# A two-block model: the delta net's chain starts 35 phases behind the forget gate's, and ScalarE copies four kinds of tiles out of PSUM

## The chip, the cores and the metric

The kernel runs on one NeuronCore of one Trainium2 chip. The metric is the device time of one launch in microseconds (us), here the median of three runs. A profiled execution gives one more time, with the span of the core and the start and duration of every instruction.

## What is computed

The reference runs two transformer blocks over 256 tokens of width 2048 in fp32. The first block is attention beside a diagonal state space model and a feed-forward net. The second block mixes three branches: a long convolution, a gated linear recurrence ("hgrn2", here the **forget gate**) and a **gated delta net**. Both recurrences have 8 heads of 128 by 128 and run in two directions, over 256 tokens of context and 256 tokens of the grid:

```python
lf_f, k_f = forget(f_f, lb_f)            # log decay and key of the forget gate
o_f, s_f = _gla_scan(qh, k_f, ih, lf_f, states[0])
o_b, s_b = _gla_scan(_flip(qh), _flip(k_b), _flip(ih), _flip(lf_b), states[1])
o = _rmsnorm_2(o_f + _flip(o_b), norm_w) * jax.nn.sigmoid(heads(g))
...
o_f, s_f = _delta_scan(q, k, v, g_f, jax.nn.sigmoid(b_f), states[0])
o_b, s_b = _delta_scan(_flip(q), _flip(k), _flip(v), _flip(g_b), _flip(jax.nn.sigmoid(b_b)), states[1])
o = _rmsnorm_2(o_f + _flip(o_b), norm_w) * jax.nn.silu(zh)
```

Both scans are done by blocks of 128 tokens: products inside a block are joined over levels of halves (64, 32, ... 1 tokens), then a state goes from block to block.

## The kernel before, in words

The program writes each engine's instruction list by hand. SyncE loads weights in tiles of 256 KB into a ring of 8 slots. Most of the time goes to projections; the change touches one stage, `heads2`, from 2533 to 3502 us of the span.

In `heads2` two chains run side by side, `forget_*` (functions for TensorE, VectorE and ScalarE) and `delta_*`. A chain is a Python generator per engine, and every `yield` ends a **phase**. `lockstep` takes one phase of each generator in turn, so it fixes the order in which every engine gets the pieces of the two chains; within a phase the forget gate's piece stands first, the end of the head before ahead of it, and both directions (r = 0, 1) follow one another. Each engine executes its list strictly in that order and waits on semaphores for the others. Nothing waits for a phase as such.

- One head of the forget gate takes 52 phases. I number them p0 to p51. Phases p0 to p10 are the **start**: bounds, the decay's reciprocals (all of p2), scans (p4), keys, their transpose and the diagonal product (p9, p10). Then 7 levels of 5 phases, then the state's steps from p46.
- One head of the delta net takes 49 phases, q0 to q48. q0 to q8 are its **opening** (products and masks); q8 to q32 are 6 **levels** of 4 phases. In a level TensorE makes `left` (8 fp32 products 128x128, 16 instructions in the trace), ScalarE keeps it in `y`, TensorE makes `both` (16 products 128x64, 32 instructions), VectorE subtracts (L1747, L1749) and masks (L1739) for the next level. q32 to q48 are the **tail**: the sides, `wide` and its negation, and four times `solved`, new values `vn`, state.
- At a head's end `end_*` normalizes its output; it runs in the first three phases of the next head.
- `beside` puts pieces of ordinary projections between the phases, the **background**: 8 groups of 36 pieces (32 of them are two products `L589`, 4 are for ScalarE's stores), spread over 414 phases.

`chain` runs the 8 heads one after the other. The delta net's chain is 18 phases late at head 0. As its head is 3 phases shorter, it is 15 late at head 1 and 3 early at head 7.

Of the kernel before, what the change touches and what calls it, by code (L numbers as in the profile page):

```python
# [10 lines left out]
ACT = mybir.ActivationFunctionType  # L11
AX = mybir.AxisListType

P = 128
# [191 lines left out]
def lockstep(strands):  # L206
    strands = list(strands)
    while strands:
        for s in list(strands):
            try:  # L210
                next(s)
            except StopIteration:
                strands.remove(s)
        yield

def beside(strand, pieces, background):
    total = sum(n for _, n in background)
    gens = [g for g, _ in background]
    done = given = 0
    for _ in strand:  # L220
        done += 1
        while gens and given < total * done / pieces:
            try:
                next(gens[0])
                given += 1
            except StopIteration:
                gens.pop(0)
    for g in gens:
        for _ in g:
            pass  # L230
# [1188 lines left out]
def tiles(b, n=NT):  # L1419
    return b[:, 0:n * P].rearrange("p (j t) -> p j t", j=n)  # L1420

def flat(t):
    return t.rearrange("p j t -> p (j t)")
# [54 lines left out]
def forget_vector(k, r, head):  # L1478
    v, s, po = k.nc.vector, k.s, k.acc[2 + r]
    h, after, before, end = hg_views(k, r)  # L1480
    fwd = r == 0
    ev = lambda name, *x: ("hg_" + name, r, head, *x)
    f, kk, e1, ks, cm, qe, att, m, st = (h[n] for n in ("f", "k", "e1", "ks", "cum", "qe", "att", "lev", "st"))
    lbc, lb1c = k.lb[:, r, head:head + 1], k.lb1_[:, r, head:head + 1]
    own = Own(k)
# [36 lines left out]
    own(v.tensor_tensor(ks, ks, kk, ALU.mult), *ev("keys"))  # L1522
    yield
    yield
    v.wait_ge(*s.at(*ev("keys_t")))
    own(v.tensor_copy(e1, tiles(po)), *ev("kst"))
    if not fwd:
        own(v.tensor_tensor(qe, end[:, 0:2, :].broadcast_to((P, 2, P)), before[:, 0:2, :], ALU.subtract), *ev("query_sums"))
    yield
# [38 lines left out]
def forget_scalar(k, r, head):  # L1568
    a, s = k.nc.scalar, k.s
    h, after, before, end = hg_views(k, r)  # L1570
    fwd = r == 0
    ev = lambda name, *x: ("hg_" + name, r, head, *x)
    yield
    a.wait_ge(*s.at(*ev("bounded")))
    a.activation(h["e1"], h["e1"], ACT.Exp).then_inc(*s.made("scalar_done", *ev("exped")))
    yield
    yield
    a.wait_ge(*s.at(*ev("scaled")))
    a.activation(h["f"], h["f"], ACT.Ln).then_inc(*s.made("scalar_done", *ev("logs")))
    yield  # L1580
    yield
    a.wait_ge(*s.at(*ev("sums")))
    a.activation(h["ks"], h["ks"], ACT.Exp).then_inc(*s.made("scalar_done"))
    a.activation(h["eend"], h["cum"][:, :, P], ACT.Exp).then_inc(*s.made("scalar_done", *ev("decays")))
    yield
    yield
    yield
    if fwd:
        a.activation(h["qe"], after[:, 0:2, :], ACT.Exp).then_inc(*s.made("scalar_done", *ev("query_decays")))
    else:  # L1590
        a.wait_ge(*s.at(*ev("query_sums")))
        a.activation(h["qe"], h["qe"], ACT.Exp).then_inc(*s.made("scalar_done", *ev("query_decays")))
    yield
    yield
    for level in range(7):
        yield
        a.wait_ge(*s.at(*ev("spans", level)))
        a.activation(h["lev"], h["lev"], ACT.Exp).then_inc(*s.made("scalar_done", *ev("span_decays", level)))
        yield
        yield  # L1600
        yield
        yield
    for _ in range(6):
        yield
# [85 lines left out]
def delta_vector(k, r, head):  # L1690
    v, s = k.nc.vector, k.s
# [4 lines left out]
    own = Own(k)  # L1696
# [57 lines left out]
    own(v.tensor_tensor(x, k.kt_h, col(ek), ALU.mult), *ev("sides"))  # L1754
    yield
    yield
    v.wait_ge(*s.at(*ev("wide")))
    own(v.tensor_scalar(y, tiles(b0), -1.0, None, ALU.mult, ALU.bypass), *ev("negated"))
    for n, j in enumerate(order_of(r)):
        yield  # L1760
        v.wait_ge(*s.at(*ev("solved", n)))
        own(v.tensor_copy(vn, b1[:, 0:P]), *ev("new", n))
        yield
        if n < 3:
            yield
            v.wait_ge(*s.at(*ev("added", n)))
            if n == 0:
                own(v.tensor_copy(st, b1[:, P:2 * P]), *ev("state", n))
            else:
                own(v.scalar_tensor_tensor(st, st, el[:, j:j + 1], b1[:, P:2 * P], ALU.mult, ALU.add), *ev("state", n))  # L1770
            yield

def delta_scalar(k, r, head):
    a, s = k.nc.scalar, k.s
    d, (g_, gc_, be, eg, el, ek), b0, b1 = dn_views(k, r)
    ev = lambda name, *x: ("dn_" + name, r, head, *x)
    yield
    yield
    yield
    yield  # L1780
    a.wait_ge(*s.at(*ev("logs")))
    a.activation(d["dec"], d["dec"], ACT.Exp).then_inc(*s.made("scalar_done"))
    a.activation(d["qe"], tiles(b0, 2), ACT.Exp).then_inc(*s.made("scalar_done"))
    a.activation(eg, gc_, ACT.Exp).then_inc(*s.made("scalar_done"))
    a.activation(el, el, ACT.Exp).then_inc(*s.made("scalar_done"))
    a.activation(ek, ek, ACT.Exp).then_inc(*s.made("scalar_done", *ev("decays")))
    yield
    yield
    yield
    yield  # L1790
    for level in range(5, -1, -1):
        yield
        yield
        a.wait_ge(*s.at(*ev("left", level)))
        a.activation(d["y"], tiles(b0), ACT.Copy).then_inc(*s.made("scalar_done", *ev("kept", level)))  # L1795
        yield
        yield
    yield
    yield
    for n in range(4):  # L1800
        yield
        yield
        if n < 3:
            yield
            yield
# [32 lines left out]
def hg_start_scalar(k, head):  # L1838
    a, s, b = k.nc.scalar, k.s, head % 2
    a.wait_ge(*s.at("hg_loaded", head))  # L1840
    if head:
        a.wait_ge(*s.at("hg_q", head - 1))
    a.activation(k.hsg, flat(k.hq[b]), ACT.Sigmoid).then_inc(*s.made("scalar_done"))
    a.activation(k.hgt[b], k.hgt[b], ACT.Sigmoid).then_inc(*s.made("scalar_done", "hg_sig", head))
    for _ in range(8):
        yield
    if head < 7:
        hg_load(k, head + 1)
# [11 lines left out]
def hg_start_vector(k, head):  # L1860
    v, s, q = k.nc.vector, k.s, flat(k.hq[head % 2])
    yield
    v.wait_ge(*s.at("hg_sig", head))
    v.tensor_tensor(q, q, k.hsg, ALU.mult).then_inc(*s.made("vector_done", "hg_q", head))
    yield
    v.wait_ge(*s.at("hg_v_t", head))
    v.tensor_copy(flat(k.hvt), k.acc[2][:, :]).then_inc(*s.made("vector_done", "hg_vt", head))
    yield

def dn_start_scalar(k, head):  # L1870
# [60 lines left out]
def chain(k, name, start, strand, end, delay=0):  # L1931

    for _ in range(delay):
        yield
    for head in range(8):
        before = [end(k, name, head - 1)] if head else []
        yield from lockstep(before + [strand(k, r, head) for r in range(2)] + [start(k, head)])
    yield from end(k, name, 7)

def heads2(k, hg_start, forget, dn_start, delta, end, whole):  # L1940
    chains = [chain(k, "hg", hg_start, forget, end), chain(k, "dn", dn_start, delta, end, 18)]
    beside(lockstep(chains), 414, [(whole(k, g), 36) for g in k.some("read", 11, 12) + k.some("gates", *range(6))])

def heads2_tensor(k):
    heads2(k, hg_start_tensor, forget_tensor, dn_start_tensor, delta_tensor, end_tensor, whole_tensor)
# [475 lines left out]
```

## Time and profile before

| | |
|---|---|
| median of 3 runs | 4931.92 us (4926.59 to 4939.75) |
| the profiled execution | 4934.87 us, its span 4933.4 us |
| TensorE matmuls busy | 4316.6 us, 87% |
| VectorE busy | 2810.2 us, 57% |
| ScalarE busy | 1548.4 us, 31% |
| `heads2` | 2533 to 3502 us |
| SyncE's weights | 597 MB in the launch, 34 MB of them in `heads2` |

Busy time is the sum of an engine's instructions. It is a mean over stages with different limits, so what matters here is read inside `heads2`. Matmuls overlap with the next one, so that a group of n is shorter than n single ones.

### The profile page before, as it was taken

Reading aid. Unit: us, or ns where it says so; the run is one execution under the profiler, and the core shown is the slowest. Engines: PE = TensorE matmul, PEld = TensorE weight load, DVE = VectorE, ACT = ScalarE, POOL = GpSimd, SP = SyncE. Lnnn points to the kernel's source line nnn. Section 1 sums busy time; section 2 is a strip of 40 time slices with the busy share of each in tenths; the row PEclk is TensorE's granted clock in tenths of the full one; section 3 lists DMA queues with packets and bytes.
Section 4 is the critical chain, followed back from the end, with each engine's and each line's share of the span. In section 5 each row is a group of like instructions: output and inputs, shape, how many; then the busy total and the mean of one; then the engine's idle time right before and its main releaser. Section 6 shows DMA issues by size and latency. Waiting matters only on the chain.

```text
span 4933.4 us, 69710 instructions
## 1 busy us (share of the span) xinstructions
PE 4316.6 (87%) x28096; PEld 3667.4 (74%) x28096; DVE 2810.2 (57%) x5619; ACT 1548.4 (31%) x2683; POOL 0.2 (0%) x4
## 2 busy tenths in 40 slices
PE   7598899699999989999877778777778897999997
PEld 7333223689999978889767777777645797999997
DVE  4756444566556542234557777777632476655654
ACT  3211111444444432234122222222100243444442
POOL 0000000000000000000000000000000000000000
PEclk9799999899999999999789899998989999999999
DMA  5344555346565654457451112121422463655653
GB/s 174 96 147 147 169 163 155 121 153 190 187 187 180 192 149 120 115 147 208 120 150 51 55 52 58 50 58 40 127 70 75 156 200 116 192 187 185 186 188 112
DMA packets 383056, 669.52 MB, mean 136 GB/s; under 512 B 43897, under 2 KB 77402, under 8 KB 382220
## 3 DMA queue, kind: packets, MB, share of 16 engines
q1 hardware_dynamic: 327168, 595.74, 40.2%
q10 hardware_dynamic: 55564, 69.31, 4.3%
q8 instruction: 221, 3.62, 0.3%
q14 instruction: 103, 0.84, 0.1%
HBM read 634.87 MB, written 29.46 MB: 135 GB/s over the span
## 4 chain that ended last, share of the span: by engine, by line
PE 63%; DVE 13%; issue 2%; ACT 2%; DMA 1%; ACTq 0%; DVEq 0%
PE acc L547 13%; PE acc L549 12%; PE acc L548 12%; PE acc L589 8%; PE bank L548 2%; PE bank L547 2%; PE bank L549 2%; PE bank L1654 2%; PE bank L1663 2%; PE bank L1661 1%; ACT weights_hi L511 1%; PE bank L2130 1%; DVE arena L1493 1%; PE acc L1462 1%; PE bank L734 1%
## 5 line engine op out<-in xcount | busy, mean ns | idle before, releaser
L526 DVE TENSOR_TENSOR weights_lo<-weights_ring,weights_hi 128x512 fp32r<-128x512 f32 x1600 | 1094.1, 691 | 1022.5 <-ACT weights_hi L511 1020.9
L511 ACT ACTIVATE weights_hi<-weights_ring 128x512 fp32r<-128x512 f32 x1600 | 994.3, 630 | 1078.8 <-PE acc L549 882.3
L548 PE MATMUL acc<-arena_halves,weights_hi 128*128 128x256 f32 (+2 forms) x3136 | 916.3, 292 | 0.0
L547 PE MATMUL acc<-arena_halves,weights_lo 128*128 128x256 f32 (+1 forms) x2944 | 860.4, 292 | 21.7 <-DVE weights_lo L526 12.2
L549 PE MATMUL acc<-arena_halves,weights_hi 128*128 128x256 f32 (+1 forms) x2944 | 858.8, 292 | 0.0
L547 PE MATMUL acc<-moving_halves,weights_lo 128*128 128x256 f32 (+1 forms) x2816 | 792.1, 281 | 73.0 <-DVE weights_lo L526 72.3
L549 PE MATMUL acc<-moving_halves,weights_hi 128*128 128x256 f32 (+1 forms) x2816 | 786.6, 279 | 0.0
L548 PE MATMUL acc<-moving_halves,weights_hi 128*128 128x256 f32 x2624 | 731.4, 279 | 0.0
L548 PEld LDWEIGHTS acc<-arena_halves,weights_hi 128*128 128x128 f32 x3136 | 590.5, 188 | 12.1
L547 PEld LDWEIGHTS acc<-moving_halves,weights_lo 128*128 128x128 f32 x2816 | 535.7, 190 | 81.6 <-DVE weights_lo L526 53.6
L589 PE MATMUL acc<-moving,weights_ring 128*128 128x256 f32 x2304 | 581.2, 398 | 10.4 <-ACT arena L692 9.3
L547 PEld LDWEIGHTS acc<-arena_halves,weights_lo 128*128 128x128 f32 x2944 | 553.3, 188 | 36.9 <-DVE weights_lo L526 13.0
L549 PEld LDWEIGHTS acc<-arena_halves,weights_hi 128*128 128x128 f32 x2944 | 553.6, 188 | 13.6
L549 PEld LDWEIGHTS acc<-moving_halves,weights_hi 128*128 128x128 f32 x2816 | 535.4, 190 | 0.0
L589 PEld LDWEIGHTS acc<-moving,weights_ring 128*128 128x128 f32 x2304 | 442.1, 201 | 95.7 <-issue 30.5
L548 PEld LDWEIGHTS acc<-moving_halves,weights_hi 128*128 128x128 f32 x2624 | 497.9, 190 | 0.0
L1088 PE MATMUL acc<-weights_ring,cc 128*2 128x512 f32 x768 | 370.6, 620 | 12.2 <-ACT mods_row L1101 12.1
L1088 PEld LDWEIGHTS acc<-weights_ring,cc 128*2 128x2 f32 x768 | 55.5, 85 | 247.6 <-issue 221.9
L548 PE MATMUL bank<-arena_halves,weights_hi 128*128 128x256 f32 (+2 forms) x640 | 209.3, 327 | 0.0
L547 PE MATMUL bank<-arena_halves,weights_lo 128*128 128x512 f32 (+1 forms) x512 | 171.8, 336 | 0.0
L549 PE MATMUL bank<-arena_halves,weights_hi 128*128 128x512 f32 (+1 forms) x512 | 171.0, 334 | 0.0
L1795 ACT ACTIVATE arena<-bank 128x512 f32<-128x512 f32 x96 | 56.6, 596 | 236.7 <-PE bank L1654 236.7
(422 smaller groups left out, 4830.9 us busy)
## 6 DMA issues: line engine op xcount, KB each, us to landing
weights_ring<-in_w_in SPq DMA_DIRECT2D x624, 256.0 KB, 2.7
weights_ring<-in_w_ff SPq DMA_DIRECT2D x512, 256.0 KB, 3.0
weights_ring<-in_w_ada SPq DMA_DIRECT2D x384, 256.0 KB, 2.9
weights_ring<-in_w_up SPq DMA_DIRECT2D x256, 256.0 KB, 2.9
weights_ring<-in_w_down SPq DMA_DIRECT2D x256, 256.0 KB, 3.2
weights_ring<-in_w_out SPq DMA_DIRECT2D x128, 256.0 KB, 3.2
weights_ring<-in_w_branch SPq DMA_DIRECT2D x96, 256.0 KB, 3.3
s_state<-arena ACTq DMA_DIRECT2D x36, 256.0 KB, 2.8
```

The source lines that it names most:

```text
L511: a.activation(whi, k.slot(g.ring0 + kc), ACT.Copy).then_inc(*s.made("scalar_done", "high", n))
L526: v.tensor_tensor(wlo, k.slot(g.ring0 + kc), whi.bitcast(F32), ALU.subtract).then_inc(*s.made("vector_done", "low", n))
L547: pe.matmul(g.out[m], wlo[:, cols], xhi, start=first, stop=False, skip_group_check=g.shared)
L548: pe.matmul(g.out[m], whi[:, cols], xlo, start=False, stop=False, skip_group_check=g.shared)
L549: mm = pe.matmul(g.out[m], whi[:, cols], xhi, start=False, stop=last, skip_group_check=g.shared)
L589: mm = pe.matmul(g.out[m], k.slot(g.ring0 + kc)[:, m * P:(m + 1) * P], g.x(kc), start=kc == 0 and m % 2 == 0, stop=last, skip_group_check= ...
L734: mm = pe.matmul(k.bank[0][:, 0:n], k.c("ones"), squares[:, c, :], start=c == 0, stop=c == chunks - 1)
L1088: mm = pe.matmul(g.out[0], ccv[:, kc, :], k.slot(g.ring0 + kc), start=kc == 0, stop=kc == g.kchunks - 1)
L1462: mm = pe.matmul(po[:, P * j:P * j + P], h["lev"][:, j, :], h["lev"][:, j, :], start=True, stop=True)
L1654: mm = pe.matmul(b0[:, P * j:P * j + P], mt[:, j, :], x[:, j, :], start=True, stop=True)
L1663: mm = pe.matmul(b1[:, 64 * j:64 * j + 64], y[:, j, :], level_columns(xt[:, j, :], level, 1 - r), start=True, stop=True)
L1795: a.activation(d["y"], tiles(b0), ACT.Copy).then_inc(*s.made("scalar_done", *ev("kept", level)))
```

## The change

Two things change, both in `heads2`.

The chains: the delta net's starts 35 phases late rather than 18, and `chain` fills each head up to 51 phases. The forget gate's heads have 52 and aren't filled. So the delta net is 35 - h phases late at head h, 28 at the last. The last phase of the stage is number 446 rather than 419, and the background is spread over 444.

The copies: the transposed keys (`kst`, 16 times 128x512), the transposed values (`hg_vt`, 8 times 128x512), the negated product (`negated`, 16 times 128x512) and the new values (`new`, 64 times 128x128) are taken out of PSUM by ScalarE's `Copy` and no longer by VectorE.

```diff
@@ forget_vector
     yield
-    v.wait_ge(*s.at(*ev("keys_t")))
-    own(v.tensor_copy(e1, tiles(po)), *ev("kst"))
     if not fwd:
@@ forget_scalar
+    a.wait_ge(*s.at(*ev("keys_t")))
+    a.activation(h["e1"], tiles(k.acc[2 + r]), ACT.Copy).then_inc(*s.made("scalar_done", *ev("kst")))
     if fwd:
@@ delta_vector
-    v.wait_ge(*s.at(*ev("wide")))
-    own(v.tensor_scalar(y, tiles(b0), -1.0, None, ALU.mult, ALU.bypass), *ev("negated"))
     for n, j in enumerate(order_of(r)):
         yield
-        v.wait_ge(*s.at(*ev("solved", n)))
-        own(v.tensor_copy(vn, b1[:, 0:P]), *ev("new", n))
         yield
@@ delta_scalar
+    a.wait_ge(*s.at(*ev("wide")))
+    a.activation(d["y"], tiles(b0), ACT.Copy, scale=-1.0).then_inc(*s.made("scalar_done", *ev("negated")))
     for n in range(4):
         yield
+        a.wait_ge(*s.at(*ev("solved", n)))
+        a.activation(d["vn"], b1[:, 0:P], ACT.Copy).then_inc(*s.made("scalar_done", *ev("new", n)))
@@ hg_start_scalar
-    for _ in range(8):
+    yield
+    yield
+    a.wait_ge(*s.at("hg_v_t", head))
+    a.activation(flat(k.hvt), k.acc[2][:, :], ACT.Copy).then_inc(*s.made("scalar_done", "hg_vt", head))
+    for _ in range(6):
         yield
@@ hg_start_vector
-    v.wait_ge(*s.at("hg_v_t", head))
-    v.tensor_copy(flat(k.hvt), k.acc[2][:, :]).then_inc(*s.made("vector_done", "hg_vt", head))
@@ chain
-        yield from lockstep(before + [strand(k, r, head) for r in range(2)] + [start(k, head)])
+        phases = 0
+        for _ in lockstep(before + [strand(k, r, head) for r in range(2)] + [start(k, head)]):
+            phases += 1
+            yield
+        for _ in range(51 - phases):
+            yield
@@ heads2
-    chains = [chain(k, "hg", hg_start, forget, end), chain(k, "dn", dn_start, delta, end, 18)]
-    beside(lockstep(chains), 414, [(whole(k, g), 36) for g in k.some("read", 11, 12) + k.some("gates", *range(6))])
+    chains = [chain(k, "hg", hg_start, forget, end), chain(k, "dn", dn_start, delta, end, 35)]
+    beside(lockstep(chains), 444, [(whole(k, g), 36) for g in k.some("read", 11, 12) + k.some("gates", *range(6))])
```

VectorE's list around the forget gate's phase p2 of head 1 (L1506 is the end of p2's second direction), of the kernel before:

```order
L1506 TENSOR_TENSOR arena<-arena 128x512
L1867 COPY arena<-acc 128x512
L1762 COPY arena<-bank 128x128 x2
L1510 SCALAR_TENSOR_TENSOR arena<-arena 128x512
L1513 SCALAR_TENSOR_TENSOR arena<-arena 128x128 x4
L1516 TENSOR_TENSOR arena<-arena 128x512
L1510 SCALAR_TENSOR_TENSOR arena<-arena 128x512
L1513 SCALAR_TENSOR_TENSOR arena<-arena 128x128 x4
L1518 COPY arena<-arena 128x512
L1770 SCALAR_TENSOR_TENSOR arena<-arena,bank 128x128 x2
```

and of the change:

```order
L1506 TENSOR_TENSOR arena<-arena 128x512
L1747 TENSOR_TENSOR arena<-arena,bank 128x32x8
L1749 TENSOR_TENSOR arena<-arena,bank 128x32x8
L1739 TENSOR_TENSOR arena<-arena,consts_sb 128x512
L1747 TENSOR_TENSOR arena<-arena,bank 128x32x8
L1749 TENSOR_TENSOR arena<-arena,bank 128x32x8
L1739 TENSOR_TENSOR arena<-arena,consts_sb 128x512
L1510 SCALAR_TENSOR_TENSOR arena<-arena 128x512
L1513 SCALAR_TENSOR_TENSOR arena<-arena 128x128 x4
L1516 TENSOR_TENSOR arena<-arena 128x512
```

Before, the delta net's tail stood beside the start (new values L1762, state L1770); now a step of its levels does.

TensorE's list at the same head, from the transpose of the values (phase p0) on. Before:

```order
L1856 MATMUL acc<-consts_sb,arena 128x128 x4
L589 MATMUL acc<-moving,weights_ring 128x256 x2
L1674 MATMUL bank<-arena 128x128
L1676 MATMUL bank<-arena 128x128
L1674 MATMUL bank<-arena 128x128
L1676 MATMUL bank<-arena 128x128
L589 MATMUL acc<-moving,weights_ring 128x256 x2
L1686 MATMUL bank<-arena 128x128 x2
```

and now:

```order
L1860 MATMUL acc<-consts_sb,arena 128x128 x4
L1654 MATMUL bank<-arena 128x128 x8
L1661 MATMUL bank<-arena 128x64 x4
L1663 MATMUL bank<-arena 128x64 x4
L1661 MATMUL bank<-arena 128x64 x4
L1663 MATMUL bank<-arena 128x64 x4
L589 MATMUL acc<-moving,weights_ring 128x256 x2
L1654 MATMUL bank<-arena 128x128 x8
L589 MATMUL acc<-moving,weights_ring 128x256 x2
L1661 MATMUL bank<-arena 128x64 x4
```

Short products of the tail's solving stood behind the transpose; now it is the delta net's `left` (L1654) and `both` (L1661, L1663).

ScalarE's list in the delta net's tail of head 0, of the change (L1598 is the exponential of the forget gate's levels, L1801 the copy of new values, L1834 to L1836 the loads of the next head):

```order
L1797 ACTIVATE arena<-bank 128x512 x2
L1801 ACTIVATE arena<-bank 128x128 x2
L1834 DMA arena<-s_kf 128x512
L1834 DMA arena<-s_qf 128x256
L1834 DMA arena<-s_kt 128x512
L1835 DMA arena<-s_vt 128x512
L1836 DMA mixed<-s_read 128x256
L1598 ACTIVATE arena<-arena 128x256 x2
L1801 ACTIVATE arena<-bank 128x128 x4
L1598 ACTIVATE arena<-arena 128x256 x2
```

Before, L1797 and L1801 weren't in it. ScalarE's list as a whole now has 124 table loads (`ACT_TABLE_LOAD`) where it had 100, since the two chains' different functions alternate more often.

## Rows read from the trace of the kernel before

**Rows 1.** Windows: the stage; busy us of each engine, clock, DMA share, GB/s
```profile
2533.00:3502.00 969.00, 745.09 (x5216) 692.65 (x5216) 733.49 (x1848) 263.50 (x505) 0.00 (x0) 0.90 0.19 55
```
**Rows 2.** Timeline, VectorE: first instruction (L1487) and p10 (L1535) of forget-gate heads 0, 1, 7
```profile
2541.27 0.76 DVE L1487 TENSOR_SCALAR arena<-arena 128x512 f32<-128x512 f32 x2
2570.52 0.42 DVE L1535 TENSOR_TENSOR arena<-acc,consts_sb 128x256 f32<-128x256 f32 x1 [0.99 <-PE acc L1453]
...
2648.55 0.75 DVE L1487 TENSOR_SCALAR arena<-arena 128x512 f32<-128x512 f32 x2
2681.82 0.41 DVE L1535 TENSOR_TENSOR arena<-acc,consts_sb 128x256 f32<-128x256 f32 x1
...
3374.78 0.75 DVE L1487 TENSOR_SCALAR arena<-arena 128x512 f32<-128x512 f32 x2
3424.74 0.42 DVE L1535 TENSOR_TENSOR arena<-acc,consts_sb 128x256 f32<-128x256 f32 x1
```
**Rows 3.** Timeline, VectorE: delta net's q0, q8, q32 (head 1), q32, q0 (heads 6, 7), stage's end
```profile
2690.18 2.12 DVE L625 TENSOR_SCALAR arena<-arena 128x4 f32<-128x4 f32 x10
...
2710.58 0.68 DVE L1736 TENSOR_TENSOR arena<-consts_sb,bank 128x512 f32<-128x512 f32 x1
...
2760.35 0.69 DVE L1753 TENSOR_TENSOR arena<-arena 128x512 f32<-128x512 f32 x1
...
3345.04 0.69 DVE L1753 TENSOR_TENSOR arena<-arena 128x512 f32<-128x512 f32 x1
...
3367.09 2.12 DVE L625 TENSOR_SCALAR arena<-arena 128x4 f32<-128x4 f32 x10
...
3495.51 0.42 DVE L1912 COPY arena<-acc 128x256 f32<-128x256 f32 x1 [1.06 <-PE acc L1470]
...
3500.95 0.42 DVE L1922 TENSOR_TENSOR moving<-arena 128x256 f32<-128x256 f32 x1
```
**Rows 4.** Timeline: phase p2 of head 2 on VectorE, and TensorE's first row behind it
```profile
2775.22 0.42 DVE L1491 TENSOR_SCALAR arena<-arena 128x512 f32<-128x512 f32 x1
...
2790.30 0.68 DVE L1867 COPY arena<-acc 128x512 f32<-128x512 f32 x1
...
2791.24 1.22 PE L1686 MATMUL bank<-arena 128*128 128x128 f32 x4 [16.74 <-DVE arena L1762]
```
**Rows 5.** Windows: a stretch in head 7's start, and one in its levels
```profile
3382.00:3390.00 8.00, 0.00 (x0) 0.00 (x0) 7.72 (x11) 3.44 (x11) 0.00 (x0) 0.50 0.00 0
...
3436.00:3448.00 12.00, 12.00 (x93) 11.52 (x91) 5.35 (x16) 2.79 (x7) 0.00 (x0) 1.00 0.21 55
```
**Rows 6.** Timeline, TensorE: `left` of both directions twice, and a quarter of `both`
```profile
2604.35 1.98 PE L1654 MATMUL bank<-arena 128*128 128x128 f32 x16
...
3413.34 3.78 PE L1654 MATMUL bank<-arena 128*128 128x128 f32 x16 [4.36 <-DVE arena L1739]
...
3455.89 1.06 PE L1661 MATMUL bank<-arena 128*128 128x64 f32 x8
```
**Rows 7.** Single lines: copies out of PSUM on VectorE and ScalarE (ns min/median/max)
```profile
L1526 DVE COPY arena<-acc x16: 681/682/692, 2566.7 to 3420.0; 128x512 f32<-128x512 f32 x16
L1762 DVE COPY arena<-bank x64: 281/291/293, 2652.3 to 3486.7; 128x128 f32<-128x128 f32 x64
L1783 ACT ACTIVATE arena<-bank x16: 363/367/367, 2582.5 to 3382.9; 128x256 f32<-128x256 f32 x16
L1795 ACT ACTIVATE arena<-bank x96: 578/597/601, 2596.2 to 3461.4; 128x512 f32<-128x512 f32 x96
```
**Rows 8.** Timeline, ScalarE: a table load and the instruction behind it
```profile
2541.97 1.28 ACT L1575 ACT_TABLE_LOAD   x1
...
2543.26 1.15 ACT L1575 ACTIVATE arena<-arena 128x512 f32<-128x512 f32 x2
```
**Rows 9.** Timeline, TensorE: the forget gate's first two level products, alone in the stage
```profile
2573.36 1.05 PE L1462 MATMUL acc<-arena 128*128 128x128 f32 x8
...
2576.84 1.05 PE L1462 MATMUL acc<-arena 128*128 128x128 f32 x8
```

## The prediction

> **What bounds the kernel now.** I read the page first, then only the stage that is touched. The stage takes 969 us, a fifth of the launch; TensorE is busy for 745 us of it, VectorE for 733 and ScalarE for 264 [rows 1]. So neither of the two busy engines is full: they take turns. The windows show how. In the forget gate's start VectorE is full and TensorE stands still; in the levels TensorE is full and VectorE is half idle [rows 5]. The cause is phase p2: one block of 15.1 us on VectorE (2790.30 less 2775.22), and as both chains share its in-order list, the delta net's small step behind it arrives late and TensorE sits idle for 16.7 us [rows 4]. To the stage it thus matters what the other chain has to do while VectorE is in the start, and whether TensorE is given work that needs no VectorE.
>
> The timeline gives the price of each piece by what lay beside it:
> - start, p0 to p10: 29.3 us alone (head 0), 33.3 over the delta net's tail (head 1), 50.0 over its opening (head 7) [rows 2]. The last heads are dear because both VectorE-heavy parts meet there.
> - opening, q0 to q8, over levels: 20.4 us, with the end of the head before. Levels, q8 to q32, over levels: 49.8 us, 2.07 a phase, with TensorE full [rows 3, 5]. Tail, q32 to the next q0, over levels: 22.1 us for 17 phases [rows 3].
>
> **The change part by part.** The chains first, as they carry the sum. With a delay of 35 - h the forget gate's p0 stands at the delta net's q17 + h. So now its start lies over *levels* of the delta net at every head, the opening lies over the forget gate's levels, and so does the tail. TensorE-heavy and VectorE-heavy parts are paired, and openings no longer meet starts.
>
> *One period of the delta net*, 51 phases, put together from these pieces:
> 1. opening over levels: 20.4 us, unchanged.
> 2. 24 phases of levels, 10 of them under the forget gate's start, so 14 at 2.07: 29.0.
> 3. tail with the two phases of filling, 19 phases at 22.1/17: 24.6.
> 4. the start over ten phases of levels, which no row shows. Bound below: VectorE's work alone. From head 1's 33.3 us I take off 1.8 for the copies that leave (two of keys and one of values, 0.68 long and about 0.6 from start to start [rows 7]) and 3.5 for the tail's own steps, and add 2.5 level steps at 2.9 (six instructions of the sizes 128x256 and 128x512), so 35.2. Bound above: 48, a little under head 7's 50.0. My value: 6 for p0 and p1 with the end, 15.1 for p2, and then TensorE. The order listing shows that it can issue `left` and `both` ahead of the block's end, but a second `left` and `both`, a third `left`, the keys' transpose, the diagonal and three background pieces stand behind it. Eight instructions take 1.06 us, 0.9 where the next ones follow [rows 6], so these are 1.8, 3.5, 1.8, 0.9, 0.9 and 2.7: 11.6 us. It comes back at half clock: while it stood idle the granted clock was 0.50, the lower level of 1.2 GHz [rows 5], and `left` took 3.78 us then against 1.98 at the full clock [rows 6]; that adds about 3. With hand-overs between three engines some 19. Sum: 40. I take 40, nearer to the lower end, since that end is worked out from a row of the same start, while the upper comes from an opening that isn't there any more.
> 5. The background is thinner, 288/444 of a piece a phase for 288/414: 0.04 us a phase where TensorE is full, so -1.0.
>
> That is 113.0. *The copies*: 16 x 0.68 for keys, 8 x 0.68 for values, 16 x 0.68 for the negation and 64 x 0.29 for new values leave VectorE, 46 us by durations [rows 7]. Those in the start are counted above. The others lie in the tail over levels, which TensorE's list fills, so VectorE's relief is worth nothing there. ScalarE gains about as much: 0.60 for 128x512, and for 128x128 between 0.19 and the 0.37 of 128x256 [rows 7], I take 0.25, so 40 us more on 264 of 969. As a link of the chain that is the same as before within 0.1 us. What is new is the queue: new values now wait behind the forget gate's exponentials, five load issues at q36 and any table load. 24 more of these at 1.28 us are 31 us of ScalarE. Eleven stand at the levels' exponential, where the delta net's opening meets levels, which VectorE bounds, and the consumer is two phases (over 4 us) later, so I charge only 1.0 us a period. Sum: **114.0 us a period**. Before it was 112.8 (676.9 us from head 1's q0 to head 7's [rows 3]), but for 49 phases rather than 51.
>
> The table loads are also where a rule speaks against this. The row shows the next activation 1.29 us after the load began, so nothing lies behind the load itself [rows 8]. The Trainium skill, "ScalarE: Activation LUTs", section "What ACT_TABLE_LOAD costs", gives 1.28 us plus a drain of 1.38, 2.66 us for a switch of sets; by an estimate from that page the 24 more would be 64 us of ScalarE rather than 31. The trace agrees on the load and shows no drain behind it.
>
> *The edges*, where extra phases cost. The forget gate now runs alone for 35 phases: the start 29.3 - 0.6, then five levels at 3.7 (its products are 3.5 us apart when alone [rows 9], with thin cover), 18.5: **47.1 us** before the delta net begins. The last head has opening 20.4, levels 49 (a quarter of them alone, so slightly under 49.8), tail alone 18.5 (22.1 less four level products of the forget gate) and the last normalization 6 (3495.5 to 3501.4 [rows 3]): **94 us**. Head 0's opening has no end beside it: -3.8.
>
> *Sum*: 47.1 + 7 x 114.0 + 94 - 3.8 = 935.3 us from the first L1487. Before it was 3501.4 - 2541.3 = 960.1 [rows 2, 3]. The difference is -24.8 us, against the profiled execution's 4934.9: **4910 us**. The median of the three runs is 3 us lower than the profiled execution, so it would be 4907; I stay with the sum's own base.
>
> The fixed loads ahead of the next head (q36 and p8) have over 15 us to land; if they were late, VectorE would wait at L1487 or at `scaled`. I see no case for it, as DMA is busy for a fifth of the stage [rows 1].
>
> **The rivals.** The total is 137.3 + 7 x period, and each us on the start is 7 us on the kernel.
>
> *A. The start over levels is VectorE's work and nothing else*, 35.2 us: TensorE hides wholly in it. For it: VectorE is 97% busy in the start [rows 5]. Against: a level goes through VectorE twice in these phases, and the half clock. -25 - 34 = -59 us: 4876.
>
> *B. The block stops the levels (the other side: slower).* In the start both chains step through VectorE's list. If each level step waits for the block and for the scans of p4 as well, so that `left` and `both` are hardly issued under p2, TensorE has 16.9 us to do behind the block at a partly halved clock, and the start is 48 us, as dear as over an opening. +56 - 25 = +31: 4966. It decides from a start of 45.7 us on, where the kernel is slower by 0.3%. For it: 16.7 us of idle TensorE at a similar place [rows 4]. Against: the order listing, with 5.3 us of products ahead of the block's end.
>
> *C. ScalarE's queue.* If all 24 table loads lie on the chain, 31 us come on top less the 7 that I charge: nearly 4934, no change. For it: new values and exponentials alternate on one in-order list in the tail. Against: ScalarE is idle for 73% of the stage [rows 1]. By the page's 2.66 us instead it would be 64 - 7 - 25 = +32 us, which the row on the load speaks against.
>
> *D. The change does not do what it says*: overlapped phases stay as long as they are. From head 1's start to head 7's there were 312 phases in 726 us, 2.33 each [rows 2]; 383 of these, 47 ahead and 36 behind give 975, +15 us: 4950. That is B in a milder form (a start near 46) and shares its chance.
>
> **How the numbers follow.** A measurement of this kernel can tell about 0.3% from no change, 15 us. My forecast (a start of 38 to 43 us, so 4896 to 4931) has 0.50; A 0.17; C 0.12; B with D 0.21. Within the forecast's band about 7 parts in 10 are faster by over 15 us (0.36), the rest the same. Faster: 0.36 + 0.17 + 0.02 of C = 0.55. Same: 0.14 + 0.10 of C = 0.24. Slower: 0.21. The range goes from 4873, just under A, to 4958, which holds D and leaves out the upper half of B.
>
> **What would show it.** The profile after should have: L1487 to L1533 (p10) near 40 us at heads 1 to 7, all alike, where it was 33 to 50; the delta net's period near 114; its first opening about 47 us after the first L1487; TensorE's idle behind p2 down from 16.7 to about 10 us. VectorE's busy time in the stage falls by about 46 us and ScalarE's rises by about 70. I am wrong if the starts take over 46 us (B), if the tail over levels takes over 28 us with TensorE waiting for ScalarE's L1801 (C), or if the opening or the plain levels change their price at all, as I carried those over from other pairings.

## The result, and the profile after

The change makes the kernel **0.24% slower**: 4949.01 us, median of 8 runs (4945.34 to 4955.16), against 4936.9 us of the kernel before on the same chip. The ratio is 1.0024, 95% interval 1.0012 to 1.0035. The profiled execution has a span of 4944.6 us, 11.2 more than before. I had forecast 25 us less.

Of the span's 11.2 us, 10.7 lie in the stage. Windows of the kernel after, the stage (columns as in [rows 1]):

```profile
2533.00:3511.00 978.00, 769.17 (x5216) 711.81 (x5216) 693.14 (x1742) 330.28 (x635) 0.00 (x0) 0.89 0.19 55
```

From the first L1487 to the end of the last normalization it took 960.1 us before and takes 970.8 now (2542.39 to 3513.16), +10.7. The copies moved as announced: VectorE's busy time fell by 40 us and ScalarE's rose by 67 [rows 1]. TensorE has the same 5216 instructions, and its busy time is 24 us more; its mean granted clock is 0.89 where it was 0.90.

The timeline of VectorE after the change shows where the phases went (L1533 is p10, L625 q0, L1736 q8, L1753 q32, as in [rows 2, 3]):

```profile
2542.39 0.76 DVE L1487 TENSOR_SCALAR arena<-arena 128x512 f32<-128x512 f32 x2
...
2590.27 2.12 DVE L625 TENSOR_SCALAR arena<-arena 128x4 f32<-128x4 f32 x10
...
2628.01 0.76 DVE L1487 TENSOR_SCALAR arena<-arena 128x512 f32<-128x512 f32 x2
...
2821.45 2.12 DVE L625 TENSOR_SCALAR arena<-arena 128x4 f32<-128x4 f32 x10
2840.70 0.69 DVE L1736 TENSOR_TENSOR arena<-consts_sb,bank 128x512 f32<-128x512 f32 x1
...
2865.95 0.76 DVE L1487 TENSOR_SCALAR arena<-arena 128x512 f32<-128x512 f32 x2
...
2909.13 0.42 DVE L1533 TENSOR_TENSOR arena<-acc,consts_sb 128x256 f32<-128x256 f32 x1
...
2913.95 0.69 DVE L1753 TENSOR_TENSOR arena<-arena 128x512 f32<-128x512 f32 x1
...
2938.74 2.12 DVE L625 TENSOR_SCALAR arena<-arena 128x4 f32<-128x4 f32 x10
...
3353.69 0.76 DVE L1487 TENSOR_SCALAR arena<-arena 128x512 f32<-128x512 f32 x2
...
3419.45 2.12 DVE L625 TENSOR_SCALAR arena<-arena 128x4 f32<-128x4 f32 x10
```

Read the same way at all heads, with the forecast beside it (us; means over seven heads):

| | before | forecast | after |
|---|---|---|---|
| forget gate alone, first L1487 to first q0 | 35.3 | 47.1 | 47.9 |
| start, p0 to p10, heads 1 to 7 | 41.0 | 40 | 40.8 |
| opening, q0 to q8 (with head 0's shorter one) | 24.2 | 19.9 | 19.6 |
| levels, q8 to q32, the start in them | 50.0 | 68.0 | **72.5** |
| tail, q32 to the next q0 | 38.7 | 24.6 + 1.0 | **26.4** |
| period of the delta net | 112.9 | 113.5 | **118.45** |
| last head, its q0 to the end | 134.3 | 94 | 93.7 |

(Before, the start lay over other parts, so that only the sums of its rows compare with the new ones. The forecast's 114.0 was to be shortened by 3.8 us once, for head 0's opening, which is 113.5 as a mean.) The edges and the mean start came out within 1 us. But the starts are not all alike, as I had forecast: they take 36.9 to 44.8 us, where it was 33.3 to 50.0. The period is 5 us over, and seven of these are the 35 us by which the sum failed.

The waits of TensorE in the stage (engine, tile, line, for whom: us in total, times, longest), first before:

```profile
PE bank L1639 <- DVE arena L1722: 61.5, 8, 25.0
PE bank L1897 <- DVE mixed L1914: 23.5, 8, 17.3
PE bank L1674 <- DVE arena L1770: 20.6, 3, 16.3
...
PE bank L1686 <- DVE arena L1762: 17.8, 2, 16.7
PE bank L1674 <- DVE arena L1768: 16.7, 1, 16.7
PE bank L1682 <- DVE arena L1762: 15.7, 2, 15.5
```

and after:

```profile
PE bank L1654 <- DVE arena L1739: 74.9, 18, 17.0
PE bank L1661 <- ACT arena L1791: 42.0, 7, 16.8
PE bank L1639 <- DVE arena L1722: 18.1, 8, 3.4
```

The openings' wait fell from 61.5 to 18.1 us, as meant. The longest idle time of TensorE around p2 has mostly changed its name: it was 15.5 to 17.3 us at heads 1 to 5, mostly in front of the tail's steps, and 25.0 and 22.0 at heads 6 and 7, in front of openings. Now it is 11.6, 17.0, 16.8, 15.4, 10.7, 14.6 and 16.8 us at heads 1 to 7, in front of `left` (L1654) or `both` (L1661): 14.7 as a mean. I had forecast 10. The block of head 3 and what follows, kernel after, timeline:

```profile
2874.82 0.42 DVE L1491 TENSOR_SCALAR arena<-arena 128x512 f32<-128x512 f32 x1
...
2889.90 0.69 DVE L1510 SCALAR_TENSOR_TENSOR arena<-arena 128x512 f32<-128x512 f32 x1
2890.01 0.63 ACT L1577 ACTIVATE arena<-arena 128x512 f32<-128x512 f32 x1 [6.91 <-DVE arena L1506]
2890.55 1.07 ACT L1791 ACTIVATE arena<-bank 128x512 f32<-128x512 f32 x2
2891.18 1.97 PE L1661 MATMUL bank<-arena 128*128 128x64 f32 x8 [16.84 <-ACT arena L1791]
```

The block is 15.08 us as before. ScalarE keeps `left` in L1791 only behind the logarithm L1577, which waits for the block's end; so `both`, which I had counted as issued under the block, starts behind it. It is the same at head 7, and at head 2 even `left` stands behind the block. At the other heads the products do run beside it: 36 of TensorE's instructions start in the block at head 1, 40 at heads 4 and 5, 12 at head 6, and TensorE idles behind them. Windows of the block of head 3 and of the 4 us behind it:

```profile
2874.82:2889.90 15.08, 0.00 (x0) 0.00 (x0) 14.60 (x20) 0.63 (x1) 0.00 (x0) 0.58 0.00 0
2891.00:2895.00 4.00, 3.82 (x18) 3.82 (x19) 3.90 (x11) 3.57 (x6) 0.00 (x0) 0.50 0.10 33
```

TensorE does nothing in this block, and behind it runs at the granted clock of 0.50, the lower level of 1.2 GHz.

### The profile page after: what moved, and what is told of

Its sections match the earlier page's. It is cut to its first block and busy times, and to the rows that moved or that the text cites. A ratio compares the mean times of both kernels' runs of the same rounds, so it can differ in the third digit from the quotient of the medians.

```text
span 4944.6 us, 69734 instructions
## 1 busy us (share of the span) xinstructions
PE 4341.5 (88%) x28096; PEld 3690.2 (75%) x28096; DVE 2772.5 (56%) x5515; ACT 1613.8 (33%) x2811; POOL 0.2 (0%) x4
## 5 line engine op out<-in xcount | busy, mean ns | idle before, releaser
L547 PEld LDWEIGHTS acc<-arena_halves,weights_lo 128*128 128x128 f32 x2944 | 552.5, 188 | 37.1 <-DVE weights_lo L526 13.3
L1654 PE MATMUL bank<-arena 128*128 128x128 f32 x768 | 108.9, 299 | 74.9 <-DVE arena L1739 74.9
```

The lines of the kernel that those rows point to most:

```text
L547: pe.matmul(g.out[m], wlo[:, cols], xhi, start=first, stop=False, skip_group_check=g.shared)
L1654: mm = pe.matmul(b0[:, P * j:P * j + P], mt[:, j, :], x[:, j, :], start=True, stop=True)
```

## Experiments

Thirteen kernels ran. "Period" is again the delta net's mean from q0 to q0, in each kernel's own trace.

### Which half of the change costs: e1_chains, e2_copies

e1 has the chains alone, e2 the copies alone.

```diff
e1: chain(..., 18) -> chain(..., 35), fill to 51 phases, background over 444; all copies on VectorE
e2: keys, values, negated product, new values on ScalarE; delay 18, no fill, 414
```

> The chains alone (35 phases behind, heads filled to 51, background over 444); all four copies stay on VectorE. Theory 1 (block and clock: in the start TensorE idles some 15 us behind p2 and comes back at half clock with dense level work; the copies matter little): ratio to before 1.001 to 1.005, delta-net period 117 to 120 us, still a long wait of TensorE behind p2. Theory 2 (ScalarE's queue: the moved copies hold up the tail and the levels): the period falls to 114 or under, ratio 0.993 to 0.998. Both: tail over levels 26.5 us if the chains do it, 24.6 if the copies did.

> The four copies alone, with the old delay of 18, no filling, background over 414. Theory 1: 12 to 15 us of VectorE relief lie in the starts, where VectorE is full, so ratio 0.996 to 0.999. Theory 2: ratio 1.002 to 1.006, with TensorE waiting for ScalarE's new values.

Measured: e1 4944.66 us, ratio 1.0021 (1.0010 to 1.0033), period 119.0. e2 4938.63 us, ratio 1.0001 (0.9992 to 1.0010), period 112.9, as before.

So the chains carry the loss, and no worth of the copies is told from nothing, where theory 1 had 0.996 to 0.999 for them: with e1's chains they take 1.1 us from the levels (73.6 to 72.5) and give 1.0 back in the tail (25.4 to 26.4).

### ScalarE's queue: e3_vn_vector, e4_scalar_order

e3 is the change with the new values taken out by VectorE again. In e4 ScalarE's pieces of a phase come in the other order, the delta net's first:

```diff
-    beside(lockstep(chains), 444, ...)
+    beside(lockstep(chains[::-1] if whole is whole_scalar else chains), 444, ...)
```

> The change, with only the new values (64 copies 128x128) back on VectorE. Theory 1: same time as the change within 0.1% (ratio to before 1.001 to 1.004), as the tail's list is TensorE's. Theory 2: the tail over levels falls from 26.5 to about 24.5 us, 15 us less than the change.

> The change, with ScalarE's list alone taking the delta net's piece of a phase before the forget gate's. At the heads where keeping `left` shares phase p3 with the logarithm, it no longer stands behind it, so TensorE's wait of up to 16.8 us for L1791 shrinks to under 5. Theory 1: those are 2 or 3 of 7 starts, TensorE then gets `both` under the block: 5 to 8 us each, ratio to the change 0.996 to 0.999. If in-phase order on ScalarE matters everywhere (theory 2): more than 25 us less than the change.

Measured: e3 4944.07 us, 1.0016 (1.0006 to 1.0026), period 118.0, tail 25.5. e4 4949.59 us, 1.0025 (1.0015 to 1.0036), period 119.1. The waits of TensorE in e4:

```profile
PE bank L1654 <- DVE arena L1739: 123.0, 18, 19.1
PE bank L1639 <- DVE arena L1722: 22.0, 8, 5.2
```

The wait for L1791 is gone from the list, and the one for VectorE has grown from 74.9 to 123.0 us, against 116.9 for the two together. At heads 3 and 7 `both` is now issued in the block (25 and 29 instructions start there, where none did), and the next `left` waits for the block's end instead; at heads 1 and 5 only 4 do, where it was 36 and 40. The 5 to 8 us a head that I had expected didn't come: the order on ScalarE decides which product waits, and hardly for how long. By e3 the new values on ScalarE (rival C) cost 0.8 us in the tail and 0.4 in the period.

### TensorE's clock: e5_clock_kept, e8_clock_kept_to_end

Products of constants into a free accumulator are put behind p2 on TensorE, to keep its clock up: 22 a head in e5, by head 27 to 40 in e8. The output does not use them.

```diff
@@ hg_start_tensor
+    yield
+    if head:
+        pe.wait_ge(*s.at("hg_o_mean", head - 1))
+    for _ in range((40, 28, 38, 38, 38, 27, 33, 38)[head]):
+        pe.matmul(k.acc[3][:, 0:T], k.ident, k.c("masks")[:, 0:T], start=True, stop=True)
+    yield
```

> The change, plus 22 products 128x256 of constants in TensorE's list at each p2, into a bank that nobody reads before it is overwritten: about 9.7 us of work that needs nothing of VectorE, in a stretch where TensorE otherwise idles 15 us. It does no useful work, it only keeps the clock. Theory 1a (the half clock behind the block is what makes the 24 phases of levels 72 us instead of 68): q8 to q32 with a start falls by 3 to 4 us, the period to about 115, ratio to before 0.996 to 0.999. Theory 1b (the idle is only the hand-over between three engines, the clock is hidden): period stays at 118 or rises, ratio 1.002 to 1.004.

> The change with dummy products behind p2 on TensorE, 27 to 40 of them by head, enough to keep TensorE at work until the block on VectorE ends (in e5_clock_kept they ended some 7 us before it, and the first group of L1661 behind still took 1.97 us and the seam was unchanged, so that run did not test the clock). Theory 'clock' (part of the long seam is the half clock after TensorE's idle): the groups of 16 products at L1654 behind the block take about 2.0 us and not 3.5 to 3.8, q8 to q32 falls from 72.5 to 68 or 69 us, period from 118.5 to 114 or 115, time 0.994 to 0.998 of the kernel before. Theory 'order of work' (VectorE's own instructions and the waits between the two chains set the seam, and the clock is hidden by them): the groups are short again but q8 to q32 stays within 1 us of 72.5 and the time within 0.1% of the change's, 1.002 to 1.003.

e5 took 4947.54 us, 1.0019 (1.0009 to 1.0029), with the change's own period, 118.45. At head 2 its products ended 6 us before the block did, and the clock had fallen again, so e5 tested nothing. The first `left` behind the block of head 2, on TensorE's timeline, in the kernel after:

```profile
2772.79 3.78 PE L1654 MATMUL bank<-arena 128*128 128x128 f32 x16 [17.04 <-DVE arena L1739]
```

The same in e5:

```profile
2766.58 3.78 PE L1654 MATMUL bank<-arena 128*128 128x128 f32 x16 [7.48 <-DVE arena L1739]
```

And in e8, where it comes as one group for each direction:

```profile
2765.90 1.16 PE L1654 MATMUL bank<-arena 128*128 128x128 f32 x8 [0.58 <-DVE arena L1739]
```

In e8 each direction's 8 instructions take 1.16 us, at the full clock. Still: e8 4942.44 us, 1.0016 (1.0007 to 1.0024), period 118.48 against the change's 118.45. But that doesn't show that the clock is hidden, since e8 kept it at some heads only. The next `left` of the same head, in e8:

```profile
2775.36 3.78 PE L1654 MATMUL bank<-arena 128*128 128x128 f32 x16 [0.73 <-DVE arena L1739]
```

It runs at the lower level: behind short waits of TensorE the clock fell 10 us after the block instead of in it. In the kernel after, this `left` took twice 1.16 us. Windows from the block's end to p10, heads 2 and 7, first in the kernel after:

```profile
2771.34:2787.01 15.67, 13.52 (x86) 12.89 (x87) 12.92 (x30) 7.53 (x16) 0.00 (x0) 0.78 0.17 54
3377.72:3398.45 20.73, 18.49 (x104) 17.42 (x104) 14.85 (x34) 7.23 (x14) 0.00 (x0) 0.72 0.10 26
```

and in e8:

```profile
2764.45:2782.54 18.09, 15.20 (x91) 13.38 (x90) 12.87 (x30) 8.00 (x16) 0.00 (x0) 0.81 0.24 74
3373.10:3390.45 17.35, 14.88 (x108) 13.10 (x106) 14.76 (x34) 7.23 (x14) 0.00 (x0) 1.00 0.12 32
```

Where the clock stayed at 1.00 (heads 4, 6, 7), this stretch is 1.2, 0.8 and 3.4 us shorter than in the change, and at head 3 (0.90 for 0.71) 1.5. Where it fell again (heads 1, 2, 5) the stretch is 1.6, 2.4 and 0.4 us longer. Over the seven heads it is 131.2 us in e8 and 133.5 in the change. So e8 shows that this filler buys nothing, and leaves open what a clock kept to the end would be worth.

### Filling the block: e6_background_in_block, e7_before_background_in_block

If TensorE idles for 15 us a head beside a block of VectorE, work that needs no VectorE belongs there. e6 (the change) and e7 (the kernel before) give 16 of a head's 36 background pieces at once at p2, the other 20 spread over 416 phases:

```diff
-def beside(strand, pieces, background):
+def beside(strand, pieces, background, bulk=0):
...
-        while gens and given < total * done / pieces:
+        now = min(bulk * ((done - 3) // 52 + 1), 8 * bulk)
+        while gens and given < now + (total - 8 * bulk) * done / pieces:
```

> The change, with the background laid differently: 16 of the 36 pieces of a head go to the forget gate's p2 (14 us of TensorE work that needs no VectorE), the other 20 are spread over its 52 phases. Theory 1: it keeps the clock as well and takes 0.26 us a phase out of the levels that fill TensorE; the period falls from 118.4 to 108 to 112, ratio 0.987 to 0.993. Theory 1b: only the thinner background counts, 5 to 6 us a period, ratio 0.994 to 0.997. If the weights' ring of 8 slots can't feed it: TensorE waits for weights in p2 and nothing is won.

> The kernel before (delay 18, copies on VectorE), with the same layout of the background. TensorE's idle behind p2 (16.7 us) is filled; the levels lose 0.24 us a phase, 24 phases: 5 to 6 us a period, and 3 us of half clock. Ratio 0.990 to 0.995. If the layout is worth more to the change (whose levels lie beside the start) than to this one, then the chains' shift was right and only the block's idle spoiled it; if it is worth the same, the shift stays a loss of 0.2%.

Measured: **e6 4868.25 us, 0.9854** (0.9839 to 0.9868); e7 4887.05 us, 0.9889 (0.9873 to 0.9904). The period falls from 118.45 to 108.3 and from 112.9 to 106.2. Both gain more than expected (0.987 to 0.993 and 0.990 to 0.995). The change's sign has turned with the layout: with the block filled in both kernels it is 19 us faster (4868.25 against 4887.05), where without that it was 12 slower.

### The rest of that layout: e9_chains_bulk16, e10_bulk20, e11_bulk20_vn_vector

e9 is e1 (copies on VectorE) with 16 pieces at p2; e10 the change with 20; e11 is e3 with 20.

> The chains alone (all copies on VectorE) with 16 of the 36 background products of a head given at p2: tells what the copies are worth once the block is filled. e6_background_in_block, with the copies on ScalarE, gave 4868 us, ratio 0.985. If the copies are worth nothing here too (levels +1.1, tail -1.0 us a period, as without the filled block) it is at 4866 to 4871. If VectorE's instructions bind more once TensorE no longer starves, the copies' 5.7 us of VectorE's work a head show and this run is 10 to 40 us slower than 4868. If the new values on ScalarE cost more than the others bring, it is faster than 4866.

> The change with 20 instead of 16 of the 36 background products of a head given at p2. In the 16 case TensorE was still idle for some us behind them. Theory 'cover': more of the block is filled, each head gains another 1 to 2 us: 4850 to 4862 us, ratio 0.981 to 0.984. Rival 'overrun': the eviction of the 20 products on ScalarE or their columns on TensorE reach past the end of the block and hold the seam back: 4870 to 4885.

> As e10_bulk20, but the new values are taken out of the bank by VectorE (the rest of the copies by ScalarE). The tail was 0.9 us a head shorter so without the filled block (e3_vn_vector), for 0.1% in all. If this holds here, 4 to 8 us faster than e10_bulk20; if VectorE's 24 extra instructions bind, 3 to 8 us slower.

Measured, on one chip (before: 4932.48 us): e9 4869.59 us, 0.9868 (0.9854 to 0.9881), period 109.3; **e10 4857.18 us, 0.9846** (0.9832 to 0.9860), period 108.7; e11 4858.56 us, 0.9851 (0.9831 to 0.9872), period 108.6. The intervals of e9 and e6 overlap, so the 0.14% between them, which would be the copies' worth here, isn't told from nothing. Nor is the place where the new values are taken out (64 instructions, not 24), where 4 to 8 us were expected. e10's 20 pieces are not told apart from e6's 16 by the intervals; its starts are 1.8 us shorter (37.9 against 39.7), its tails 1.2 longer, and its stage is as long (887.0 against 886.8 us). Windows of the block of the same head as above, in e10:

```profile
2845.19:2860.27 15.08, 15.08 (x71) 13.29 (x70) 14.60 (x20) 0.63 (x1) 0.00 (x0) 1.00 0.58 148
```

The block takes 15.08 us beside a full TensorE too, and the granted clock stays at 1.00.

### Is it the background or the phases: e12_no_background, e13_before_no_background

Both kernels with all 288 pieces behind the stage, so that only the two chains are in it.

```diff
-    beside(lockstep(chains), 444, ...)
+    beside(lockstep(chains), 444000, ...)
```

> The change with the 288 projection pieces of the stage all behind it rather than beside it. Only the two chains remain in the stage; the time as a whole must be longer, since the projections are no longer hidden. Read is the period of the delta net, against the same edit of the kernel before (e13). Theory 'background' (the two chains alone pair as well as forecast; what was missed is that projection pieces stand in TensorE's way in more phases than before): the period here is at most 2 us longer than e13's, for 51 phases against 49, e.g. 100 against 98. Rival 'phases' (the overlapped start is dear in itself, for instance because the levels go through VectorE behind the block): the period stays 4 to 6 us longer than e13's, as it is with the background (118.45 against 112.93).

> The kernel before with the 288 projection pieces behind the stage. Gives the delta net's period without background, 49 phases: with 36 pieces a head it is 112.93 us, with 16 of them in the block 106.2. Both theories expect 95 to 102 us here; the difference to e12_no_background decides between them (up to 2 us, or 4 to 6). Time as a whole longer than before: 288 pieces at about 0.97 us are 280 us, less what the stage gets shorter (8 times 11 to 15 us).

The delta net's first and last q0 in e12, from VectorE's timeline:

```profile
2580.61 2.12 DVE L625 TENSOR_SCALAR arena<-arena 128x4 f32<-128x4 f32 x10
...
3339.28 2.12 DVE L625 TENSOR_SCALAR arena<-arena 128x4 f32<-128x4 f32 x10
```

The same two in e13:

```profile
2574.59 2.12 DVE L625 TENSOR_SCALAR arena<-arena 128x4 f32<-128x4 f32 x10
...
3297.81 2.11 DVE L625 TENSOR_SCALAR arena<-arena 128x4 f32<-128x4 f32 x10
```

A seventh of each difference is the period: 108.4 us for 51 phases in e12, 103.3 for 49 in e13. The difference is 5.1 us, almost the 5.5 with the background. So the theory "background" falls and "phases" holds: the two chains alone cost 5 us more a period, two phases longer, when paired so, where 1.2 was forecast (114.0 against 112.8). The clock is not the same in the two: the mean granted clock from the first L1487 to the end of the last normalization is 0.80 in e12 and 0.83 in e13, so that a part of the 5 us may be the clock's. (As a whole: e12 5110.96 us, 1.0336, 1.0321 to 1.0352; e13 5097.27, 1.0325, 1.0304 to 1.0346.) The stage without background is 10.1 us longer than e13's, against the 10.7 with it.

These two runs also say what the background costs. Spread over the phases its 36 pieces take 10.1 us of a period of the change (118.45 less 108.4) and 9.6 of the kernel before. In e6 the period is as long with all of its background as without any: 108.3, and the stage is 886.8 us against 891.2. In e7 2.9 us a period remain. By the stage, the change was 10.7 us longer than the kernel before and is now 22.3 shorter (886.8 against 909.1). Of these 33 us, 24 are the period's and 8 the last head's, which fell from 93.7 to 83.5 us in the change and from 134.3 to 131.8 in the kernel before.

Two things beside the filled block are in that comparison. The granted clock is higher with the background: its mean over the stage is 0.94 in e6 against 0.80 in e12, so "as long as without" is a net result. And the layout takes table loads away: ScalarE's list has 124 in the change and 102 in e6, but 100 in both the kernel before and e7. The 22 loads are 28 us of ScalarE at 1.28 each, 3.5 us a head, as much as e6's period gained beyond e7's (10.1 less 6.7). So no run shows whether the filled block alone turns the sign. e10, with 114 loads and 4 more pieces in the block, has the same stage as e6.

## Why the prediction was wrong

**What held.** The lead of 47.1 us (47.9), the opening over levels (20.4, with head 0's 19.9; 19.6), the last head (94; 93.7), the start (40; 40.8), and that nothing outside the stage moves. A part of the mechanism was right as well: openings no longer meet starts, and the last head is 40 us shorter. That all starts would be alike was not: they spread over 8 us, half as far as before.

**What failed is the sum for one period**, by 5 us, in two of its steps:

1. *"24 phases of levels, 10 of them under the forget gate's start, so 14 at 2.07: 29.0"*, with the 1.0 of step 5 off: 28.0. The 14 phases take 72.5 - 40.8 = 31.7 us (half a us more, as at head 7 p10 comes 3.5 us behind q32). Without background they take 67.1 - 39.6 = 27.5, 1.96 each, where e13's levels, without a start in them, take 41.5/24 = 1.73. So some 3 us come with the pairing and not with the background, the clock's part included. My cut was too sharp: I let the dear stretch begin at L1487 and end at p10. The row of the end of a head shows what lies before it:

```profile
2864.68 0.42 DVE L1914 COPY arena<-acc 128x256 f32<-128x256 f32 x1 [3.27 <-PE acc L1470]
2865.14 0.42 DVE L1915 TENSOR_TENSOR arena<-acc,arena 128x256 f32<-128x256 f32 x1
2865.60 0.42 DVE L1916 TENSOR_TENSOR arena<-arena 128x256 f32<-128x256 f32 x1
2865.95 0.76 DVE L1487 TENSOR_SCALAR arena<-arena 128x512 f32<-128x512 f32 x2
```

   These three instructions are 1.3 us in front of every start, and VectorE stands in front of them for the forget gate's last output for up to 4.1 us, where before it was 1.5 at most. In e12 that wait is 2.15 us at heads 3, 4 and 7 and none at the others, 0.9 as a mean, so that the end of a head makes up to 2.2 of the 3 us. I take the rest to lie in the phases behind p10; no run takes the parts from each other. The 1.0 of step 5 (a thinner background) never appeared: the background costs 10.1 us a period, and 9.6 before.

2. *"19 phases at 22.1/17: 24.6"*, a price taken from the last two heads. It is 25.4 with the chains alone, 26.4 with the new values on ScalarE, 1.0 of which I had charged.

That is +3.7 and +0.8 a period; with the start's 0.8, it is 5.3, less 0.3 for the opening: 5.0 us, seven times over. (The prediction's 22.1/17 for 19 phases is 24.7, not 24.6.)

**The start was right in its mean, and partly by luck.** I let TensorE idle for some 10 us and put 11.6 us of products, 3 for the half clock and hand-overs behind the block. TensorE idles for 14.7 us as a mean, at three of the seven heads it issues nothing during the block, and still the start is 40.8. Whether TensorE gets work done beside the block hardly shows in it: the starts of those three heads (2, 3, 7) are 36.9, 43.2 and 44.8 us, of the others 41.4, 40.0, 42.1 and 37.1. An idle time that was 5 us too short must have been made up for by a term that was too long; no run says by which. The 3 us for the clock are neither confirmed nor refuted by e8.

**The rivals.** D forecast 4950 us, from 2.33 us for each overlapped phase. From head 1's L1487 to head 7's there are 312 phases again, and they take 3353.69 - 2628.01 = 725.7 us, where it was 726.2 [rows 2]. So the average phase is as dear as it was, and the change pays for the phases that it adds. The pair without background agrees: two phases more at e13's average, 103.3/49 = 2.11, are 4.2 of the 5.1 us. D happened in its number, but not by the mechanism that I lent it, a start near 46: I had tied it to B, and gave both together 0.21. A falls (start 35.2). B falls (48). C's queue is worth 0.8 us a head in the tail, near the 1.0 charged, and all that is over in the tail is 0.8 us a period. The 24 more table loads come with the chains: e1 has them with the copies on VectorE, e2 does not with the copies on ScalarE. But the two chains' functions alone, the reason that I gave with the change, do not make them: without background the lists have 101 (e12) and 97 (e13). Of the 24, 11 are at the levels' exponential and 5 at the background's stores (L692), whose functions come between. In e12 23 of the 124 loads are gone, in e13 3 of 100, and the difference of the periods only falls from 5.5 to 5.1. So, as far as two runs at different clocks can tell, the loads are not the change's loss; their price by themselves stays open.

The Trainium skill ("ScalarE: Activation LUTs", section "What ACT_TABLE_LOAD costs") states a drain behind a load, and by an estimate from that page the 24 would be 64 us. The trace after shows none either. A load between two activations on ScalarE, kernel after:

```profile
3017.31 0.60 ACT L1791 ACTIVATE arena<-bank 128x512 f32<-128x512 f32 x1 [1.05 <-PE bank L1654]
3017.92 1.28 ACT L692 ACT_TABLE_LOAD   x1
3019.22 0.39 ACT L692 ACTIVATE arena<-acc 128x256 f32<-128x256 f32 x1
```

What I should have weighed: D asks for no piece prices. An average over 312 phases stood against a sum of five prices, each of them taken from another pairing.

## What to carry to other kernels

When one engine has a block of 15 us that the other chain must wait for, shifting the chains mostly changes which instruction waits behind it; to gain, give the waiting engine work in its list there that needs nothing of the busy one. The same background that cost 10 us a head when spread evenly cost nothing on balance when 16 of its 36 pieces stood beside the block, with a higher clock and fewer table loads beside. Check a filler run by the clock of the whole stretch, not of the first instruction alone: the fall may only have moved. And when a forecast is a sum of prices read in other pairings, set the plain average (time per phase in the overlapped stretch) beside it, and let the difference have a large chance.

## What the runs showed of the hardware

TensorE's lower clock was easy to see: `left` took 3.78 us behind 17 us of idle time and twice 1.16 when TensorE had been kept at work. Its price is less easy: in e8 the stretch behind the block was 0.8 to 3.4 us shorter at the three heads where the clock stayed at 1.00, and 0.4 to 2.4 us longer at the three where it fell 10 us later, with the same period (118.45 and 118.48). Work that ended 7.5 us before `left`, in e5, did not keep the clock: 3.78 us again. And VectorE's block was not slowed at all by a full TensorE and 148 GB/s of transfers beside it: 15.08 us in both. The copies out of PSUM took 0.28 us on ScalarE (128x128, 64 times), against 0.29 on VectorE [rows 7].
